# Last turn of two MLPs written out, and the norms behind them done inside the MLP stage

## The chip, the core and the metric

The kernel runs on one core of a Trainium2 chip. The metric is device time in microseconds (us), the median of several executions. Engines are named as in the profile: PE is TensorE's matrix multiplications, PEld its weight loads, DVE is VectorE, ACT is ScalarE, POOL is GpSimd, SP is the engine that issues most loads. Work on one engine runs in the order in which it is written; engines wait for each other only through semaphores.

## What is computed

A residual stream `x` of 256 rows by 1024 columns passes through a first network of two layers (attention, then a gated linear attention that is called gla below, each followed by a squared-ReLU MLP of width 4096) and a second network of two layers (a mix of attention and convolution, then a product-key mixture of experts). Of this, the change touches the end of each MLP and the norm behind it:

```python
def rmsnorm(x, g):
    y = x32 * lax.rsqrt(jnp.mean(x32 * x32, axis=-1, keepdims=True) + EPS)
    return (y * g.astype(jnp.float32)).astype(x.dtype)
...
        h = h + sq_relu_mlp(rmsnorm(h, norm_mlp[i]), mlp_w_in[i], mlp_w_out[i])
    return rmsnorm(h, final_norm)
...
        h = rmsnorm_2(x, norm1_g[l]) * (1.0 + sc1) + sh1
        proj = h @ w_in[l]
```

Behind the first MLP comes one norm (`norm_mix[1]`). Behind the second come two in a row: `final_norm`, whose result is the new `x`, and on it the first norm of the second network with its scale and shift.

## The kernel before

The kernel is a row of stages. Each has its own tiles and semaphores, and between two stages all engines meet in a barrier (L136). The 256 rows of `x` are two tiles (`t` = 0, 1) of 128 partitions. Weights come by SP in panels of 2 MB into a ring of four slots. A product of float32 accuracy is made of three passes (`three_passes`, L190 to L194): each operand is split into `hi`, a rounded copy by ACT, and `lo`, the rest, by DVE (`rest_of`, L187).

`mlp` (L414) handles the 32 chunks of 128 hidden columns in TURNS = 4 turns of CH = 8 chunks, in a hardware loop `Fori` on each engine. For a chunk `c`, `first(c)` multiplies the input weights with the turned input `hT` into the PSUM bank `hid[c % 2]` (24 matmuls of 256 columns). ACT takes the ReLU, DVE squares it to `act2`, ACT and DVE split that to `hidden`. `second(c)` multiplies `hidden` with the output weights into `acc`, four banks for tile and column half `(t, b)`, in 12 matmuls of 512 columns: three passes for each of the four `(t, b)`. PE's order is `first(c)`, `second(c - 2)`. The output weights of a chunk are split into buffer `c % 2` of `second_w`, so ACT waits until `second(c - 2)` has used it (the wait on `act_used` ahead of L566). `acc` starts with `x` itself (L509), so that it ends as the new residual stream.

Beside that, DVE sums rows for the conditioning of the second network (`condition`, L611), with rows that POOL loads, three in two chunks. After the last turn it stores them (`K.ada`, L628, L630), SP writes them out (L486), and in the second MLP DVE prepares the modulation row `K.mod[:, 0]` (L633). SP loads the next stage's four panels (`following`) as the slots fall free.

When the last `second` is done, ACT copies tile 1 of `acc` to `K.x` (L579) and DVE tile 0 (L636), and the stage ends. After the first MLP a stage `norm` (L235) follows: sum of squares of tile 1 on ACT and of tile 0 on DVE, mean, root, inverse, scaling by the gain row (L290), then for each of four halves (tile and column half) four PE transposes through PSUM (L309), ACT's `hi` (L273) and DVE's `lo` (L187) into `hT`. The next stage is `gla`. After the second MLP the stage `between_blocks` (L313, "bridge" in the trace) does two norms in a row: the same as `norm` up to the inverse, then `K.x` scaled (L357), the squares again (L339), mean, root, inverse again, the scaling by `K.mod[:, 0]` (L366), the shift by `K.mod[:, 1]` (L371), transposes (L384), `hi` (L345) and `lo`. The next stage is `mix`.

`Tail` (L642) is a norm done inside a stage: attention and gla end with it. There tile 0's norm is done while PE still sums tile 1, and tile 0's transposes are issued between the last matmuls of tile 1.

## Time and profile before

| | us |
|---|---|
| median of 3 runs | 2418.85 (2417.86 to 2419.85) |
| the profiled execution, device time | 2418.26 |
| its span, first to last instruction | 2416.6 |
| PE busy | 2112.2 (87%) |
| DVE busy | 1600.4 (66%) |
| ACT busy | 807.5 (33%) |
| mean granted clock of PE | 0.95 |
| the first MLP in the trace, with the norm behind it | 141.7 to 347.1 |
| the second MLP, with the two norms behind it | 504.7 to 712.3 |

All times in the rows are in microseconds from the start of the span. PE's granted clock is given as a share of full speed: 1.00 is the level of 2.4 GHz, 0.50 that of 1.2 GHz, a value between them a stretch that has both. The ends of matmuls are modelled, so distances between starts are safer than durations.

### The profile page before, as it was taken

Reading aid. Unit: us, or ns where it says so; the run is one execution under the profiler, and the core shown is the slowest. Engines: PE = TensorE matmul, PEld = TensorE weight load, DVE = VectorE, ACT = ScalarE, POOL = GpSimd, SP = SyncE. Lnnn points to the kernel's source line nnn. Section 1 sums busy time; section 2 is a strip of 40 time slices with the busy share of each in tenths; the row PEclk is TensorE's granted clock in tenths of the full one; section 3 lists DMA queues with packets and bytes.
Section 4 is the critical chain, followed back from the end, with each engine's and each line's share of the span. In section 5 each row is a group of like instructions: output and inputs, shape, how many; then the busy total and the mean of one; then the engine's idle time right before and its main releaser. Section 6 shows DMA issues by size and latency. Waiting matters only on the chain. (4 is left out here: it accounts for less than half of the span.)

```text
span 2416.6 us, 24918 instructions
## 1 busy us (share of the span) xinstructions
PE 2112.2 (87%) x8768; PEld 1363.8 (56%) x8768; DVE 1600.4 (66%) x3308; ACT 807.5 (33%) x1740; POOL 563.4 (23%) x604
## 2 busy tenths in 40 slices
PE   6689989989979999998788777899998988788777
PEld 5478877778969766554233333497664543333333
DVE  6567864577875658667766775656486676667655
ACT  4544435444445523221122112346232212121222
POOL 0000010000000203333333333102033333343332
PEclk9889989999989999999999989899999998898999
DMA  7068863178864449999999999864399999999997
GB/s 277 5 255 318 297 231 114 70 292 322 299 238 168 152 145 417 422 423 421 422 422 422 422 421 423 343 251 153 136 403 422 422 422 423 422 422 422 422 422 307
DMA packets 161333, 772.71 MB, mean 320 GB/s; under 512 B 12967, under 2 KB 13351, under 8 KB 89550
## 3 DMA queue, kind: packets, MB, share of 16 engines
q0 software_dynamic: 80640, 587.24, 59.1%
q1 hardware_dynamic: 80590, 184.17, 21.1%
q8 instruction: 56, 0.92, 0.2%
q14 instruction: 47, 0.39, 0.0%
HBM read 770.27 MB, written 1.10 MB: 319 GB/s over the span
## 5 line engine op out<-in xcount | busy, mean ns | idle before, releaser
L2667 ACT ACTIVATE experts_diagonal<-ident,experts_weight 128x128 f32<-128x128 f32 x488 | 155.9, 390 | 639.2 <-DVE experts_weight L2544 629.1
L2810 PE MATMUL experts_fourth<-ring,experts_diagonal 128*128 128x512 f32 x464 | 226.5, 638 | 45.0 <-ACT experts_diagonal L2667 41.7
L2288 POOL DMA_INDIRECT ring<-in_experts_uv_dram,experts_at x196 | 186.7, 953 | 305.3 <-PE experts_fourth L2810 142.1
L187 DVE TENSOR_TENSOR mix_lo<-ring,mix_hi 128x1024 fp32r<-128x1024 f32 (+1 forms) x98 | 132.5, 1358 | 118.2 <-ACT mix_hi L1962 115.1
L2489 DVE CUSTOM_DVE_ANT_0 ring<-ring,experts_second 128x1024 f32<-128x1024 f32 x116 | 141.6, 1220 | 96.5 <-DMA ring<-in_experts_uv_dram,experts_at 95.8
L2288 POOL DMA_INDIRECT experts_v_slot<-in_experts_uv_dram,experts_at x160 | 154.2, 964 | 204.5 <-PE experts_fourth L2810 108.1
L2810 PEld LDWEIGHTS experts_fourth<-ring,experts_diagonal 128*128 128x128 f32 x464 | 91.6, 203 | 176.4 <-issue 106.0
L2810 PE MATMUL experts_fourth<-experts_v_slot,experts_diagonal 128*128 128x512 f32 x320 | 156.2, 629 | 34.0 <-ACT experts_diagonal L2667 33.9
L2810 PE MATMUL experts_first<-ring,experts_diagonal 128*128 128x512 f32 x320 | 155.7, 636 | 33.5 <-ACT experts_diagonal L2667 33.5
L2810 PE MATMUL experts_first<-experts_v_slot,experts_diagonal 128*128 128x512 f32 x320 | 150.7, 611 | 13.5 <-ACT experts_diagonal L2667 13.4
L192 PE MATMUL mlp_hid<-mix_hT_hi,mlp_in_hi 128*128 128x256 f32 x512 | 147.2, 288 | 5.9 <-DVE mlp_in_lo L187 5.9
L494 POOL DMA_DIRECT2D mlp_ada_rows<-in_ada_turned_dram x48 | 25.6, 533 | 536.2 <-DVE mlp_turn_sums L611 315.7
L193 PE MATMUL mlp_hid<-mix_hT_lo,mlp_in_hi 128*128 128x256 f32 x512 | 146.0, 285 | 0.0
L194 PE MATMUL mlp_hid<-mix_hT_hi,mlp_in_lo 128*128 128x256 f32 x512 | 145.9, 285 | 0.0
L2489 DVE CUSTOM_DVE_ANT_0 experts_v_slot<-experts_v_slot,experts_second 128x1024 f32<-128x1024 f32 x80 | 97.6, 1221 | 69.2 <-DMA experts_v_slot<-in_experts_uv_dram,experts_at 68.7
L1962 ACT ACTIVATE mix_hi<-ring 128x1024 fp32r<-128x1024 f32 (+1 forms) x96 | 99.7, 1049 | 116.4 <-PE mix_sums L194 106.0
L2489 DVE CUSTOM_DVE_ANT_0 ring<-ring,experts_third 128x1024 f32<-128x1024 f32 x80 | 97.6, 1220 | 60.9 <-DMA ring<-in_experts_uv_dram,experts_at 60.2
L2489 DVE CUSTOM_DVE_ANT_0 experts_v_slot<-experts_v_slot,experts_third 128x1024 f32<-128x1024 f32 x80 | 97.5, 1219 | 57.3 <-DMA experts_v_slot<-in_experts_uv_dram,experts_at 56.4
L2810 PEld LDWEIGHTS experts_fourth<-experts_v_slot,experts_diagonal 128*128 128x128 f32 x320 | 63.5, 203 | 122.9 <-issue 74.9
L2810 PEld LDWEIGHTS experts_first<-ring,experts_diagonal 128*128 128x128 f32 x320 | 63.3, 202 | 115.8 <-issue 74.7
L611 DVE CUSTOM_DVE_ANT_0 mlp_ada_rows<-mlp_ada_rows,mlp_c_row 128x1024 f32<-128x1024 f32 x96 | 117.2, 1221 | 6.3 <-DMA mlp_ada_rows<-in_ada_turned_dram 6.3
L2662 ACT ACTIVATE experts_dots<-experts_dots 128x4 f32<-128x4 f32 x122 | 25.1, 205 | 278.5 <-DVE experts_dots L2489 278.4
(487 smaller groups left out, 4982.9 us busy)
## 6 DMA issues: line engine op xcount, KB each, us to landing
mlp_ada_rows<-in_ada_turned_dram POOLq DMA_DIRECT2D x48, 1024.0 KB, 5.4
ring<-in_w_in_dram SPq DMA_DIRECT2D x20, 2048.0 KB, 8.8
ring<-in_mlp_w_in_dram SPq DMA_DIRECT2D x16, 2048.0 KB, 9.8
ring<-in_mlp_w_out_dram SPq DMA_DIRECT2D x16, 2048.0 KB, 9.7
ring<-in_gla_w_in_dram SPq DMA_DIRECT2D x6, 2048.0 KB, 8.0
ring<-in_w_query_dram SPq DMA_DIRECT2D x6, 2048.0 KB, 8.0
ring<-in_w_out_dram SPq DMA_DIRECT2D x4, 2048.0 KB, 8.2
ring<-in_attn_w_qkv_dram SPq DMA_DIRECT2D x3, 2048.0 KB, 11.9
```

The costliest lines, as they stand in the source:

```text
L187: return dve.tensor_tensor(out_lo, a, hi.bitcast(F32), ALU.subtract)
L192: pe.matmul(out, at(lhs.hi), to(rhs.hi), start=start, stop=False, **more)
L193: pe.matmul(out, at(lhs.hi), to(rhs.lo), start=False, stop=False, **more)
L194: return pe.matmul(out, at(lhs.lo), to(rhs.hi), start=False, stop=stop, **more)
L494: pool.dma_start(ada_rows[:, slot, :, :], src).then_inc(ada_in[slot], 16)
L611: dve.tensor_tensor_reduce(a, a, c_row[:], 1.0, 0.0, ALU.mult, ALU.add, turn_sums[:, step:step + 1]).then_inc(summed, 1)
L1962: act.activation(w.hi[:, p % BUFFERS, begin:PIECE], K.ring[:, i % SLOTS, c * PIECE + begin:(c + 1) * PIECE], ACT.Copy).then_inc(hi_done, 1)
L2288: pool.indirect_dma_start(pair(i), None, rows, bass.IndirectOffsetOnAxis(ap=at[:, n, j:j + 1], axis=0)).then_inc(pair_in[slot_of(i)], 16)
L2489: dve.tensor_tensor_reduce(u_row(i), u_row(i), h2_ps[n // PH], 1.0, 0.0, ALU.mult, ALU.add, dots[:, n, j:j + 1]).then_inc(dots_done, 1)
L2662: act.activation(some, some, ACT.Gelu_apprx_tanh).then_inc(gelu_done, 1)
L2667: act.activation(diagonal[:, i % TOPK, :], K.ident[:], ACT.Copy, scale=weight[:, n, i % TOPK:i % TOPK + 1]).then_inc(diagonal_ready, 1)
L2810: mm = pe.matmul(y[n // PH][:, b, :], diagonal[:, j, :], v_row(i)[:, b * HALF:(b + 1) * HALF], start=n % PH == 0 and j == 0, stop=False, s ...
```

## The change

In both MLPs the loops run over three turns, and the fourth is written out. `second_w` has four buffers in place of two, in all turns. In the fourth turn PE does `second` for chunks 0 to 3 as before, but keeps chunks 4 to 7 until all of `first` is done. Then it goes through these four chunks for tile 0 (both column halves), again for tile 1's left half, and again for its right half.

A new class `Ending` does the norm or the norms in the MLP stage. It reads `acc` in PSUM where the stages before read `K.x`. With one norm (`again` false) the transposes of tile 0 are issued ahead of the last chunk's matmuls of tile 1; with two (`again` true) they follow all matmuls. With two norms, `K.x` first becomes `acc` times the gain row of the first norm ("weighed"), the second sum of squares is taken of that, and the first inverse is multiplied in later: into the second inverse for `hT` (`both`), and on ACT into `K.x` (`normalise`). The stages `norm` behind the first MLP and `between_blocks` go, with their barriers. DVE's preparation of `K.mod[:, 0]` stands ahead of the last turn, and so does its wait for the gain rows.

```diff
+class Ending:
...
+    def __init__(self, st, K, acc, hid, dead, hT, row, again):
+        self.K, self.acc, self.hid, self.hT, self.row, self.again = K, acc, hid, hT, row, again
+        self.more = st.ps("more", [P, 2, HALF])
+        self.xn = st.sb("xn", [P, T, D])
+        if again:
+            spare = st.sb("spare", [P, 2, HALF])
+            self.spare = [[a.rearrange("p a n -> p (a n)") for a in dead], [spare[:, h, :] for h in range(2)]]
...
+    def sums(self, t, f=0, n=D):
+        return self.acc[:, t, :, :].rearrange("p b n -> p (b n)")[:, f:f + n]
+
+    def bank(self, n):
+        return (self.hid, self.more)[n // 2][:, n % 2, :]
+
+    def transposes(self, pe, t):
+        for h in range(2):
+            pe.wait_ge(self.xn_done, 2 * t + h + 1)
+            for k in range(4):
+                f = (4 * h + k) * P
+                mm = pe.transpose(self.bank(2 * t + h)[:, k * P:(k + 1) * P], self.xn[:, t, f:f + P], self.K.ident[:])
+            mm.then_inc(self.turned, 1)
...
+    def scalar(self, act):
+        def square(t, part, n=HALF):
+            f = part * HALF
+            act.wait_ge(self.summed, 1 if t == 0 else 2 + part)
+            if self.again and (t, part) != (0, 1):
+                act.wait_ge(self.weighed, 1 if t == 0 else 3 + part)
+            to = self.spare[t][part] if self.again else self.xn[:, t, f:f + n]
+            act.activation(to, self.sums(t, f, n), ACT.Square,
+                           accum_out=self.ssq[:, 0, t, part:part + 1]).then_inc(self.squared, 1)
+
...
+        def normalise(t):
+            act.wait_ge(self.rstd_done, t + 1)
+            act.wait_ge(self.scaled, 2 * t + 2)
+            act.activation(self.K.x[:, t, :], self.K.x[:, t, :], ACT.Copy, scale=self.rstd[:, 0, t:t + 1])
+
+        if self.again:
+            square(0, 1)
+            square(0, 0)
+            square_weighed(0, 0, D, 0, 2)
+            root(0, 0, 1)
+            root(0, 1, 2)
+            square(1, 0)
+            square_weighed(1, 0, HALF, 0, 3)
+            normalise(0)
+            square(1, 1)
+            root(1, 0, 3)
+            high(0)
+            root(1, 1, 4)
+            high(1)
+            normalise(1)
+        else:
+            square(0, 0, D)
+            root(0, 0, 1)
+            square(1, 0)
+            act.wait_ge(self.xn_done, 2)
+            act.activation(self.K.x[:, 0, :], self.sums(0), ACT.Copy)
+            high(0)
+            high(1)
+            square(1, 1)
+            root(1, 0, 2)
+        high(2)
+        high(3)
+        if not self.again:
+            act.wait_ge(self.xn_done, 4)
+            act.activation(self.K.x[:, 1, HALF:D], self.sums(1, HALF, HALF), ACT.Copy)
...
+    def vector(self, dve, own):
+        def weigh(t, f, part):
+            dve.wait_ge(self.summed, 1 if t == 0 else 2 + part)
+            if (t, part) == (0, 1):
+                dve.wait_ge(self.squared, 1)
+            dve.tensor_tensor(self.K.x[:, t, f:f + HALF], self.sums(t, f, HALF), self.row[:, f:f + HALF],
+                              ALU.mult).then_inc(self.weighed, 1)
+
...
+        def mean_again(t, parts, squares):
+            dve.wait_ge(self.squared2, squares)
+            r = self.rstd[:, 0, t:t + 1]
+            own(dve.tensor_scalar(self.whole[:, 1, t:t + 1], total(1, t, parts), r, r, ALU.mult, ALU.mult))
+            dve.tensor_scalar(self.ms[:, 1, t:t + 1], self.whole[:, 1, t:t + 1], 1.0 / D, EPS, ALU.mult,
+                              ALU.add).then_inc(self.ms_done, 1)
...
+        if self.again:
+            weigh(0, 0, 0)
+            weigh(0, HALF, 1)
+            mean(0, 2, 2)
+            inverse(0, 0, 1)
+            mean_again(0, 1, 1)
+            inverse(0, 1, 2)
+            both(0)
+            scaled_again(0, 0)
+            weigh(1, 0, 0)
+            scaled_again(0, HALF)
+            weigh(1, HALF, 1)
+            square_weighed(1, HALF, 1)
+            mean(1, 2, 4)
+            shifted(0, 0)
+            inverse(1, 0, 3)
+            mean_again(1, 2, 2)
+            shifted(0, HALF)
+            inverse(1, 1, 4)
+            both(1)
+            scaled_again(1, 0)
+            scaled_again(1, HALF)
+            shifted(1, 0)
+            shifted(1, HALF)
+            low(0)
+            low(1)
+        else:
+            mean(0, 1, 1)
+            inverse(0, 0, 1)
+            scaled(0, 0)
+            scaled(0, HALF)
+            dve.wait_ge(self.squared, 2)
+            dve.tensor_copy(self.K.x[:, 1, 0:HALF], self.sums(1, 0, HALF))
+            low(0)
+            low(1)
+            mean(1, 2, 3)
+            inverse(1, 0, 2)
+            scaled(1, 0)
+            scaled(1, HALF)
+        low(2)
+        low(3)
...
+    BUFFERS = 4
+    HELD = CH - BUFFERS
...
-        first_w, second_w = (Parts(st.mem, nc, f"{st.name}_{n}", [P, 2, PIECE]) for n in ("in", "out"))
+        first_w, second_w = (Parts(st.mem, nc, f"{st.name}_{n}", [P, buffers, PIECE])
+                             for n, buffers in (("in", 2), ("out", BUFFERS)))
...
+        ending = Ending(st, K, acc, hid, (relu[:], act2[:]), hT, rows[0][0], scale is not None)
...
-                pe.sem_inc(act_used, LAG)
...
+                pe.sem_inc(act_used, BUFFERS)
...
+                def second(i, c, parts):
+                    pe.wait_ge(hidden_split, i * CH + c + 1)
+                    pe.wait_ge(out_split, i * CH + c + 1)
+                    for t, b in parts:
+                        mm = three_passes(pe, acc[:, t, b, :], hidden, second_w,
+                                          lambda x: x[:, c % 4, t * P:(t + 1) * P],
+                                          lambda x: x[:, c % BUFFERS, b * HALF:(b + 1) * HALF],
+                                          start=False, stop=False, skip_group_check=True)
+                    return mm
+
+                every = [(t, b) for t in range(T) for b in range(2)]
+                with pe.Fori(0, TURNS - 1) as i:
                     for c in range(CH + LAG):
                         if c < CH:
-                            first(c)
+                            first(i, c)
                         if c >= LAG:
-                            second(c - LAG)
+                            second(i, c - LAG, every).then_inc(act_used, 1)
+
+                last = TURNS - 1
+                for c in range(CH):
+                    first(last, c)
+                    if LAG <= c < HELD + LAG:
+                        second(last, c - LAG, every).then_inc(act_used, 1)
+                for c in range(HELD, CH):
+                    mm = second(last, c, every[0:2])
+                mm.then_inc(ending.summed, 1)
+                for c in range(HELD, CH):
+                    mm = second(last, c, every[2:3])
+                mm.then_inc(ending.summed, 1)
+                pe.wait_ge(relu_done, CH * TURNS)
+                for c in range(HELD, CH):
+                    mm = second(last, c, every[3:4])
+                    if c == CH - 2 and scale is None:
+                        ending.transposes(pe, 0)
+                mm.then_inc(ending.summed, 1)
+                if scale is not None:
+                    ending.transposes(pe, 0)
+                ending.transposes(pe, 1)
...
-                        act.wait_ge(act_used, i * CH + (c + 1 - 2 + LAG))
-                        act.activation(second_w.hi[:, c % 2, :], raw_out(g, m), ACT.Copy).then_inc(out_hi, 1)
...
+                    act.wait_ge(act_used, i * CH + c + 1)
+                    act.activation(second_w.hi[:, c % BUFFERS, :], raw_out(g, m), ACT.Copy).then_inc(out_hi, 1)
...
-                act.wait_ge(act_used, CH * TURNS + LAG)
-                act.activation(K.x[:, 1, :], acc[:, 1, :, :].rearrange("p b n -> p (b n)"), ACT.Copy)
...
+                with act.Fori(0, TURNS - 1) as i:
+                    turn(i)
+                turn(TURNS - 1)
+                ending.scalar(act)
...
+                with dve.Fori(0, TURNS - 1) as i:
+                    turn(i)
+                    keep(i)
+                dve.wait_ge(K.rows_in, 16 * len(rows))
                 if scale is not None:
                     dve.wait_ge(K.rows_in, 16 * (1 + len(rows)))
                     own(dve.scalar_tensor_tensor(out=K.mod[:, 0, :], in0=scale, scalar=1.0, in1=K.mod[:, 0, :],
                                                  op0=ALU.add, op1=ALU.mult))
-                dve.wait_ge(act_used, CH * TURNS + LAG)
-                own(dve.tensor_copy(K.x[:, 0, :], acc[:, 0, :, :].rearrange("p b n -> p (b n)")))
+                turn(TURNS - 1)
+                keep(TURNS - 1)
+                dve.tensor_tensor(K.ada[:, layer, :], K.ada[:, layer, :], ada_bias[:], ALU.add).then_inc(added, 1)
+                ending.vector(dve, own)
...
-    norm(nc, K, hT=hT, there=memory.shared[:, 0, :])
...
-    between_blocks(nc, K, A, memory)
```

Not shown: `first`, `rectify`, `square`, `condition` and the turns of ACT and DVE keep their content and take the turn as an argument.

## Rows read from the trace of the kernel before

**Rows 1.** Waits of PE, first MLP (engine, line waited for: us, times, longest).
```profile
PE mlp_hid L192 <- DVE mlp_in_lo L187: 4.2, 4, 3.2
PE mlp_acc L509 <- PEq L136: 2.3, 1, 2.3
```

**Rows 2.** Who waited for the tile `mlp_hidden_lo` in both MLPs (us in total, times).
```profile
PEld mlp_acc L192: 3.6, 8
```

**Rows 3.** Timeline of the first MLP's last turn: start, duration, engine, line, [idle before].
```profile
327.19 0.40 PE L192 MATMUL mlp_acc<-mlp_out_hi,mlp_hidden_hi 128*128 128x512 f32 x1
327.39 0.38 ACT L558 ACTIVATE mlp_relu<-mlp_hid 128x256 f32<-128x256 f32 x1 [1.50 <-PE mlp_hid L194]
...
329.94 0.39 PE L192 MATMUL mlp_acc<-mlp_out_hi,mlp_hidden_hi 128*128 128x512 f32 x1
330.14 1.06 ACT L566 ACTIVATE mlp_out_hi<-ring 128x1024 fp32r<-128x1024 f32 x1 [2.36 <-PE mlp_acc L194]
...
332.38 0.42 DVE L187 TENSOR_TENSOR mlp_hidden_lo<-mlp_act,mlp_hidden_hi 128x256 fp32r<-128x256 f32 x1
332.44 0.39 PE L194 MATMUL mlp_acc<-mlp_out_hi,mlp_hidden_lo 128*128 128x512 f32 x1
...
332.85 0.50 PE L192 MATMUL mlp_acc<-mlp_out_hi,mlp_hidden_hi 128*128 128x512 f32 x1
...
333.18 0.39 PE L193 MATMUL mlp_acc<-mlp_out_lo,mlp_hidden_hi 128*128 128x512 f32 x1
```

**Rows 4.** Timeline from the first MLP's last matmul to gla's first.
```profile
335.48 0.39 PE L194 MATMUL mlp_acc<-mlp_out_hi,mlp_hidden_lo 128*128 128x512 f32 x1
...
347.14 0.37 SPq L850 DMA_DIRECT2D gla_wz<-in_gla_w_in_dram  x1
...
350.05 0.80 PE L192 MATMUL gla_sums<-gla_hi,mix_hT_hi 128*128 128x512 f32 x1 [5.04 <-DVE gla_lo L187]
```

**Rows 5.** Timeline from the second MLP's last matmul to mix's first.
```profile
694.57 0.39 PE L194 MATMUL mlp_acc<-mlp_out_hi,mlp_hidden_lo 128*128 128x512 f32 x1
...
695.07 1.23 DVE L636 COPY x<-mlp_acc 128x1024 f32<-128x1024 f32 x1 [1.55 <-PE mlp_acc L194]
697.27 1.03 ACT L333 ACTIVATE bridge_tp<-x 128x1024 f32<-128x1024 f32 x1 [1.26 <-PEq L136]
...
701.82 1.03 ACT L339 ACTIVATE bridge_tp<-x 128x1024 f32<-128x1024 f32 x1
...
703.00 0.17 DVE L360 TENSOR_SCALAR bridge_ms<-bridge_ssq 128x2 f32<-128x2 f32 x1 [1.21 <-ACT bridge_tp L339]
703.20 0.20 ACT L342 ACTIVATE bridge_std<-bridge_ms 128x2 f32<-128x2 f32 x1 [0.23 <-DVE bridge_ms L360]
703.43 0.17 DVE L362 RECIPROCAL bridge_rstd<-bridge_std 128x2 f32<-128x2 f32 x1 [0.27 <-ACT bridge_std L342]
703.63 1.42 DVE L366 SCALAR_TENSOR_TENSOR bridge_xn<-x,bridge_rstd,mod 128x512 f32<-128x512 f32 x2
...
707.49 1.29 DVE L371 TENSOR_TENSOR bridge_xn<-bridge_xn,mod 128x512 f32<-128x512 f32 x2
...
712.34 0.34 SPq L1816 DMA_DIRECT2D mix_conv_cols<-in_conv_turned_dram  x1
```

**Rows 6.** Timeline of attention's tail, which norms tile 1 inside its stage.
```profile
131.55 1.03 PE L682 MATMUL attn_more<-ident,mod 128*128 128x128 f32 x8
...
135.22 0.63 ACT L689 ACTIVATE shared<-x 128x512 f32<-128x512 f32 x1 [1.46 <-DVE x L717]
...
135.98 0.21 DVE L721 TENSOR_SCALAR attn_tail_ms<-attn_tail_ssq 128x1 f32<-128x1 f32 x1 [0.79 <-ACT shared L689]
136.23 0.15 DVE L723 TENSOR_SCALAR attn_tail_ms<-attn_tail_ms 128x1 f32<-128x1 f32 x1
...
140.03 0.69 DVE L187 TENSOR_TENSOR mix_hT_lo<-attn_more,mix_hT_hi 128x512 fp32r<-128x512 f32 x1 [0.35 <-ACT mix_hT_hi L698]
```

**Rows 7.** Stretches: us, busy us of PE, PEld, DVE, ACT, POOL, granted clock, DMA share, GB/s.
```profile
350.00:353.50 3.50, 3.46 (x8) 2.81 (x9) 2.98 (x4) 2.80 (x3) 3.14 (x6) 0.50 0.14 44
```

275 lines of the change are left out of this document (126 added, 149 removed).

## The prediction

> **What bounds the kernel now.** I read the views in this order: the busy shares, the waits of PE inside an MLP, the timeline of an MLP's last turn, and then the timeline from its last matmul to the first matmul of the next stage. The shares say that PE is busy 87% of the span, but that is an average, and the change touches two places only.
>
> Inside the MLPs PE is the bound. From the start of the first MLP to its end PE's matmuls wait 4.2 us for split input weights, 3.2 of it once at the start, and 2.3 us at the entry barrier, and for nothing else [rows 1]. A further, small wait is booked to the weight loads: eight times, once in each turn of both MLPs, 3.6 us in total, for the `lo` part of the hidden chunk [rows 2]. What it costs is read from the distances between matmul starts. Ahead of the last `second`, the distance from L194 to L192 is 332.85 - 332.44 = 0.41 us and the next one 333.18 - 332.85 = 0.33, where the pitch is (329.94 - 327.19) / 12 = 0.229 [rows 3]. So one such wait costs 0.41 + 0.33 - 0.46 = 0.28 us. Its cause stands in the same rows: the split of the last output chunk (L566) starts at 330.14, after ACT had waited 2.36 us for PE to free one of two buffers, though the ReLU of that chunk had begun at 327.39.
>
> Behind the MLPs the norms are the bound, and PE stands still. From the last matmul's end (335.48 + 0.39 = 335.87) to the first instruction of gla (347.14) it is 11.27 us [rows 4]. From the second MLP's last matmul's end (694.96) to the first instruction of mix (712.34) it is 17.38 us [rows 5]. Both stretches lie whole on the path, as no engine has work of another stage in them. So the gain to be had is what of these 28.65 us can be done beside PE's own last matmuls, plus two of the barriers, plus the eight small waits.
>
> **The small waits.** With four buffers the split of output chunk 7 needs no release by PE. It can start when ACT is through with its ReLU, at about 327.39 + 0.3 instead of 330.14. `hidden_lo`, which ended near 332.8, then ends 2 us earlier or more and before PE comes to it at 332.67. All eight waits go: 8 x 0.28 = 2.2 us, 1.1 for each MLP. What is late next is PE itself, whose chunk pair takes 24 + 12 matmuls whatever the buffers do. In the written-out turn the order is different, so I check it apart. Let F be the end of the last `first`. PE goes straight on with chunks 4, 5 and 6 for tile 0, three times 6 x 0.229 = 1.37 us, and comes to chunk 7 at F + 4.1. DVE must by then have done, from the ReLU of chunk 6 on (F - 2.7, because the last two `first` now run back to back): a square, two condition sums, two output splits, a second square and two hidden splits. With the waits for ACT in between I come to F + 3.8. That is 0.3 us of slack: I cost this at nothing, and if the slack is gone it costs the difference, at most the 0.28 of before.
>
> **The end of the first MLP.** Let Z be the time when tile 0 is complete, after 4 x 6 x 0.229 = 5.5 us of held chunks. The remaining matmuls of tile 1 take another 5.5 us, so PE's sums without any insertion would end at Z + 5.5, which is the point that answers to 335.87. Tile 0: square of 1024 columns, mean, root, inverse, and two scalings take 1.2 + 0.63 + 2 x 0.71 = 3.3 us (lengths as in [rows 5]: 701.82 to 703.00, 703.00 to 703.63, and the halves of 1.42). PE comes to tile 0's transposes at Z + 4.8, so they wait for nothing. The eight transposes cost PE 1.03 us, read from attention's tail, which issues eight in the same place [rows 6]. The last sum is thus ready at Z + 6.55. From here on tile 1 is alone, and attention's tail shows this very chain: from the square of the last half (135.22) to the end of the last `lo` (140.03 + 0.69) it takes 5.50 us [rows 6]. The stage ends near Z + 12.1. The barrier I take as the one between the second MLP and the bridge, 696.30 to 697.27, 0.97 us [rows 5]. gla starts at Z + 13.1, that is 7.6 us after the point that answers to 335.87, against 11.27 before. Gain 3.65 us.
>
> **The end of the second MLP.** Here tile 0's chain is longer. Up to the first scaling by the product of both inverses: a weighing of 0.7, the second one with its square behind the first (to Z + 1.5), the square of the weighed tile (1.2), root, inverse, two small operations, root, inverse, the product (0.2 to 0.25 each by [rows 5, 6]): Z + 4.3. Then DVE's list goes: scale, weigh, scale, weigh (2 x 0.71 + 2 x 0.69) and a sum of squares of half a tile (0.75): Z + 7.9. ACT needs until Z + 8.95 for its two squares, `normalise` of tile 0 (1.0) and the last square (0.76), so DVE waits 1.1 us here. The second mean takes 0.4, shift 0.65, five small operations 0.9, shift 0.65, two more 0.5, giving Z + 12.1; scale twice (1.4), shift twice (1.3) and four `lo` (4 x 0.68 = 2.7) bring Z + 17.5. Transposes and `hi` run beside these. With 0.97 for the barrier mix starts at Z + 18.5, which is 13.0 us after PE's sums, against 17.38. Gain 4.4 us. Of that, what the trace of before does not show is how often DVE and ACT wait for each other in this new order. The bound from below is DVE without any wait: 1.1 us here and about 2 us ahead of Z + 4.3 fall away, 3 us better. The bound from above is another 0.27 us (the hand-over from ACT to DVE in [rows 5]) at each of some nine crossings, 2.5 us worse. I take the middle, as the list itself is fixed and its lengths are measured.
>
> **What is moved.** The preparation of `K.mod[:, 0]`, 1.2 us of DVE, now stands between turns three and four. DVE has just gained 2 us there, as its last `lo` of the turn no longer waits, so PE does not see it. Without that cover it would cost up to 1.2 us once. Its wait for the rows has nothing queued that matters: they were loaded at the start of the stage. SP's four panel loads and the store of `K.ada` hang on the splits, which come 2 us earlier. The last store is issued with nothing behind it. POOL's loads wait for the condition sums, which are not held up. The copies of `acc` to `K.x` (about 1 us each, ACT and DVE) leave the path; ACT's last one runs beside the last `lo`.
>
> **The barrier** after an MLP with nothing shorter ahead of it may be 0.8 to 1.4 us instead of 0.97. That is -0.2 to +0.4 for each.
>
> **The sum.** 2 x 1.1 + 3.65 + 4.4 = 10.3 us. The profiled execution took 2418.26, so 2408.0. It lies 0.59 us under the median of the runs shown, so the median should be 2408.6.
>
> **The code itself.** Each turn back in the loop is a jump. The starts of PE's matmuls show no idle time at any of them: the only waits of PE between the second turn and the end are for data [rows 1, 2]. By the Trainium skill (Runtime: NRT & Kernel Launch, Instruction fetch mechanics) fetching is sequential, and a taken jump to a page outside the window stalls. By it the change would save one such stall for each MLP and engine, and written-out code would cost nothing; the row has zero for the stall, so the sum stays as it is either way.
>
> **Rivals.**
> (a) *The second ending is bound by its order.* DVE and ACT hold each other up at each step of the interleaved list, for instance a root that sits on ACT behind a `hi` that waits for transposes. At most its whole gain of 4.4 us is given back: 2413.0. For it speaks that DVE's list has no free work to fill a wait with; against it that every piece is shorter than the one it replaces.
> (b) *The four buffers don't do what they say.* The eight waits stay, since the split of the hidden chunk hangs on ReLU and square and not on the buffer: 2408.6 + 2.2 = 2410.8. Against it: the 2.36 us wait in [rows 3].
> (c) *The clock stays up.* gla's first 3.5 us run at a granted clock of 0.50 [rows 7], from its first matmul at 350.05 on, after PE had been nearly idle since 335.87. If the shorter pause keeps the clock at 1.00, half of that is saved, 1.75 us, and about as much at mix: 2405. Against it: PE still pauses for more than 5 us ahead of gla's first matmul (2.9 us of it inside gla, 347.14 to 350.05).
> (d) *Slower: the written-out turn starves for instructions.* Behind the loop each engine runs into code that it has not run before, while DMA is loaded with panels. The nearest row for a sequencer that is not ready is 2.3 us at the stage's entry [rows 1]. The gain is used up when such a stall hits PE more than four times in total (10.3 / 2.3); with four in each MLP, one for each two `first`, it is 8 x 2.3 - 10.3 = 8.1 us slower: 2427. Against it: the rest of the kernel is straight code of the same kind, and PE's matmuls in it wait for data.
>
> **How the numbers follow.** Forecast 0.67, (a) 0.13, (b) 0.10, (c) 0.06, (d) 0.04. Around 2408.6 the bounds are: second ending -3 and +2.5, barriers -0.4 and +0.8, the product-key stages' own variation about 1 us as in the three runs. They do not all fall on one side, so 2404 to 2411.5 for the forecast alone; (a) and (b) are taken in up to 2413. Range 2404 to 2413. The limit of what can be told from no change is 0.2%, 4.8 us, so faster means under 2414.0. That holds for the forecast, (b), (c) and nearly all of (a): 0.92. Same 0.04, slower 0.04.
>
> **What would show it.** In the profile after: no wait of PE's weight loads for `mlp_hidden_lo` but perhaps in the last turn; the stretch from PE's last sum of the first MLP to gla's first instruction near 6.5 us (7.6 less the inserted transposes), and from that of the second MLP to mix's first near 13; the time from mix's start to the end of the span unchanged within 1 us. Wrong would be: an idle PE between the last `first` and the held chunks, a wait of DVE of more than 1.5 us in the second ending, or a stage behind that grows by what was gained.

## The result, and the profile after

The changed kernel takes 2406.49 us (2405.42 to 2408.01) against 2418.85 of the kernel before in the same runs: a ratio of 0.995, 95% interval 0.9939 to 0.996. That is 12.4 us less; the interval of the ratio stands for 9.7 to 14.8. The profiled execution took 2405.89, 12.37 less than that of before. The forecast was 10.3 less, 2408.6. The time lies inside the range, and the sign was right.

The page of the kernel after begins so (span; then busy time of an engine, its share and its instructions):

```profile
span 2404.1 us, 24851 instructions
...
PE 2102.4 (87%) x8768; PEld 1358.2 (56%) x8768; DVE 1597.4 (66%) x3321; ACT 807.4 (34%) x1755; POOL 564.8 (23%) x604
```

To see where the time went, I cut both profiled executions at the first instruction of each stage. All numbers are us; "before" and "after" are the two profiles.

| stretch | before | after | difference |
|---|---|---|---|
| first MLP's first matmul to gla's first instruction | 205.44 | 198.28 | -7.16 |
| gla | 157.56 | 157.58 | +0.02 |
| second MLP to mix's first instruction | 207.64 | 201.54 | -6.10 |
| mix to the end of the span | 1704.26 | 1705.00 | +0.74 |

The gain sits in the two MLPs and is not given back behind them. Inside an MLP the starts of the ReLUs cut it finer, since there is one for each output chunk. "Turn 1, chunk 1 to turn 3, chunk 6" holds two of the three turn ends, the row ahead of it the other one. The last column but one is the whole ending, up to the next stage's first instruction, with the last turn's own small wait in it.

| MLP | stage start to the third ReLU | third ReLU to turn 1, chunk 1 | to turn 3, chunk 6 | to the next stage | sum |
|---|---|---|---|---|---|
| first, before | 20.09 | 42.36 | 117.62 | 25.37 | 205.44 |
| first, after | 17.89 | 42.03 | 117.03 | 21.33 | 198.28 |
| second, before | 16.14 | 42.40 | 117.62 | 31.48 | 207.64 |
| second, after | 16.29 | 42.04 | 117.03 | 26.18 | 201.54 |

**The turns.** These are the two ReLUs around the end of turn 0 in the first MLP (start, duration, line, operation; in brackets the idle time ahead of it), first of before, then of after:

```profile
189.90 0.38 ACT L558 ACTIVATE mlp_relu<-mlp_hid 128x256 f32<-128x256 f32 x1 [1.50 <-PE mlp_hid L194]
201.28 0.38 ACT L558 ACTIVATE mlp_relu<-mlp_hid 128x256 f32<-128x256 f32 x1 [5.37 <-PE mlp_hid L194]
```
```profile
187.69 0.38 ACT L699 ACTIVATE mlp_relu<-mlp_hid 128x256 f32<-128x256 f32 x1 [3.98 <-PE mlp_hid L194]
198.75 0.38 ACT L699 ACTIVATE mlp_relu<-mlp_hid 128x256 f32<-128x256 f32 x1 [7.53 <-PE mlp_hid L194]
```

The distance falls from 11.38 to 11.06, 0.32 us a turn end. The waits of PE's matmuls and weight loads in the first MLP of after answer to [rows 1] and [rows 2] (time in total, times, longest):

```profile
PE mlp_hid L192 <- DVE mlp_in_lo L187: 4.0, 4, 3.2
...
PE mlp_more L363 <- DVE mlp_xn L457: 2.4, 1, 2.4
...
PE mlp_hid L192 <- ACT mlp_relu L699: 0.4, 1, 0.4
```
```profile
PEld mlp_hid L192 <- DVE mlp_in_lo L187: 5.5, 4, 3.4
...
PEld mlp_more L363 <- DVE mlp_xn L457: 3.1, 2, 2.8
```

No wait for `mlp_hidden_lo` is left in either list.

**The first ending.** The timeline of after, from the last `first` on. It answers to [rows 3] and [rows 4]:

```profile
321.33 0.40 PE L192 MATMUL mlp_acc<-mlp_out_hi,mlp_hidden_hi 128*128 128x512 f32 x1
...
326.80 0.39 PE L192 MATMUL mlp_acc<-mlp_out_hi,mlp_hidden_hi 128*128 128x512 f32 x1
327.00 1.03 ACT L373 ACTIVATE mlp_xn<-mlp_acc 128x1024 f32<-128x1024 f32 x1 [2.95 <-PE mlp_acc L194]
...
331.56 1.03 PE L363 MATMUL mlp_hid<-ident,mlp_xn 128*128 128x128 f32 x8
...
332.89 0.40 PE L194 MATMUL mlp_acc<-mlp_out_hi,mlp_hidden_lo 128*128 128x512 f32 x1
333.33 0.60 ACT L373 ACTIVATE mlp_xn<-mlp_acc 128x512 f32<-128x512 f32 x1
...
338.11 0.69 DVE L187 TENSOR_TENSOR mix_hT_lo<-mlp_more,mix_hT_hi 128x512 fp32r<-128x512 f32 x1 [0.42 <-ACT mix_hT_hi L387]
339.98 0.37 SPq L1004 DMA_DIRECT2D gla_wz<-in_gla_w_in_dram  x1
```

From 321.33 to 326.80 PE starts 24 held matmuls in 5.47 us, 0.228 each, so it does not starve in the written-out part. Z is again the time when tile 0 is complete, the end of the last of these 24. It is 326.97, and the tile is squared at once, while PE still has 5.5 us of tile 1 ahead. The transposes of tile 0 wait for nothing. The last `lo` ends at 338.80 = Z + 11.8, and gla starts at Z + 13.0.

**The second ending.** Its timeline, which answers to [rows 5], and two of the waits of DVE from Z = 681.26 on:

```profile
681.30 1.49 DVE L431 TENSOR_TENSOR x<-mlp_acc,shared 128x512 f32<-128x512 f32 x2 [1.49 <-PE mlp_acc L194]
...
685.42 0.75 DVE L467 SCALAR_TENSOR_TENSOR mlp_xn<-x,mlp_whole,mod 128x512 f32<-128x512 f32 x1
...
688.07 1.14 ACT L393 ACTIVATE x<-x,mlp_rstd 128x1024 f32<-128x1024 f32 x1
...
689.11 0.58 ACT L373 ACTIVATE mlp_spare<-mlp_acc 128x512 f32<-128x512 f32 x1
...
689.88 0.16 DVE L437 TENSOR_TENSOR mlp_whole<-mlp_ssq 128x1 f32<-128x1 f32 x1 [1.11 <-ACT mlp_spare L373]
...
691.79 0.60 ACT L387 ACTIVATE mix_hT_hi<-mlp_hid 128x512 fp32r<-128x512 f32 x1 [1.32 <-PE mlp_hid L363]
692.28 0.19 ACT L383 ACTIVATE mlp_std<-mlp_ms 128x1 f32<-128x1 f32 x1
692.51 0.16 DVE L447 RECIPROCAL mlp_rstd<-mlp_std 128x1 f32<-128x1 f32 x1 [0.32 <-ACT mlp_std L383]
...
697.61 0.69 DVE L187 TENSOR_TENSOR mix_hT_lo<-mlp_more,mix_hT_hi 128x512 fp32r<-128x512 f32 x1 [0.16 <-ACT mix_hT_hi L387]
699.10 0.34 SPq L1968 DMA_DIRECT2D mix_conv_cols<-in_conv_turned_dram  x1
```
```profile
DVE mlp_rstd L447 <- ACT mlp_std L383: 1.5, 3, 0.9
...
DVE mlp_whole L437 <- ACT mlp_spare L373: 1.1, 1, 1.1
```

The last `lo` ends at 698.30 = Z + 17.0, and mix starts at Z + 17.8. The written order costs in two places. DVE stands 1.1 us because ACT's `normalise` of tile 0 (688.07) is queued ahead of the last square (689.11). Then it stands 0.32 us for tile 1's second root (692.28): its mean was ready at 691.59, but on ACT the root is queued behind the first `hi` of tile 0 (691.79), and that waits for PE's transposes. How long they take hangs on the clock. These are the four transposes of after, then of the kernel with the later `normalise`, which is among the experiments:

```profile
690.88 0.87 PE L363 MATMUL mlp_hid<-ident,mlp_xn 128*128 128x128 f32 x4 [4.18 <-DVE mlp_xn L473]
```
```profile
691.14 0.66 PE L363 MATMUL mlp_hid<-ident,mlp_xn 128*128 128x128 f32 x4 [3.21 <-DVE mlp_xn L473]
```

In after the granted clock falls from 1.00 to 0.50 while they run, and they take 0.87 us; in the other profile it falls later, they take 0.66, and DVE does not wait for that root.

**What is left over.** Turn ends and endings give 1.87 + 4.04 + 5.30 = 11.2 us. The last piece is the first turn of the first MLP, 20.09 against 17.89, and this piece the change does not explain. In these two profiles PE idles there once for 3.2 us, for a split input weight. In both kernels the reason is the same: DVE's first condition sum stands in front of that split and waits for its rows. The timeline of after, then three stretches of before and two of after (us, busy time and instructions of PE, PEld, DVE, ACT, POOL, then the granted clock, DMA share, GB/s):

```profile
151.11 1.23 DVE L756 CUSTOM_DVE_ANT_0 mlp_ada_rows<-mlp_ada_rows,mlp_c_row 128x1024 f32<-128x1024 f32 x1 [3.91 <-DMA mlp_ada_rows<-in_ada_turned_dram]
...
152.26 1.22 DVE L187 TENSOR_TENSOR mlp_in_lo<-ring,mlp_in_hi 128x1024 fp32r<-128x1024 f32 x1
```
```profile
152.00:153.30 1.30, 0.03 (x1) 0.03 (x1) 1.30 (x4) 0.35 (x1) 0.00 (x0) 0.54 0.05 19
153.30:155.00 1.70, 1.70 (x8) 1.70 (x9) 1.70 (x4) 0.42 (x1) 0.00 (x0) 0.50 0.02 5
155.00:157.00 2.00, 2.00 (x11) 2.00 (x11) 2.00 (x3) 0.00 (x0) 0.53 (x1) 0.50 0.47 66
```
```profile
153.30:155.00 1.70, 1.47 (x12) 1.47 (x13) 1.70 (x5) 0.42 (x1) 0.00 (x0) 1.00 0.02 5
155.00:157.00 2.00, 2.00 (x19) 2.00 (x19) 2.00 (x2) 0.29 (x2) 0.53 (x1) 1.00 0.14 25
```

In before TensorE comes back from the pause at a granted clock of 0.50, its lower level of 1.2 GHz, and starts 11 matmuls in 2 us; in after it stays at 1.00, 2.4 GHz, and starts 19. Whether that belongs to the change is a question for the experiments.

### The profile page after: what moved, and what is told of

Its sections match the earlier page's. It is cut to its first block and busy times, and to the rows that moved or that the text cites. A ratio compares the mean times of both kernels' runs of the same rounds, so it can differ in the third digit from the quotient of the medians.

```text
span 2404.1 us, 24851 instructions
## 1 busy us (share of the span) xinstructions
PE 2102.4 (87%) x8768; PEld 1358.2 (56%) x8768; DVE 1597.4 (66%) x3321; ACT 807.4 (34%) x1755; POOL 564.8 (23%) x604
## 5 line engine op out<-in xcount | busy, mean ns | idle before, releaser
L2962 PE MATMUL experts_fourth<-ring,experts_diagonal 128*128 128x512 f32 x464 | 220.9, 625 | 47.5 <-ACT experts_diagonal L2819 44.1
```

Of the source, the lines that this page charges most:

```text
L2962: mm = pe.matmul(y[n // PH][:, b, :], diagonal[:, j, :], v_row(i)[:, b * HALF:(b + 1) * HALF], start=n % PH == 0 and j == 0, stop=False, s ...
```

## The experiments

My theory: the gain has three independent parts (four buffers, tile 0's norm under tile 1's matmuls, stages dropped), and the clock in the first turn is chance. Rivals: the recorded (a), (b) and (d); that dropping the stages is the gain and the held chunks are not; and that the first turn's clock belongs to the change. Eleven runs follow: nine new kernels, and each of the two once more. Each has the kernel before beside it on the same chip, and every ratio is taken to that one and not to the 2418.85 of the result. Its medians there were 2421.77 us for the first four runs, 2419.35 for the next four and 2418.91 for the last three. The ratio is an estimate from all executions, so it can differ a little from the quotient of the medians.

### Four buffers alone

```diff
-    first_w, second_w = (Parts(st.mem, nc, f"{st.name}_{n}", [P, 2, PIECE]) for n in ("in", "out"))
+    first_w, second_w = (Parts(st.mem, nc, f"{st.name}_{n}", [P, buffers, PIECE])
+                         for n, buffers in (("in", 2), ("out", 4)))
...
-    act.wait_ge(act_used, i * CH + (c + 1 - 2 + LAG))
+    act.wait_ge(act_used, i * CH + c + 1)
```

> The kernel before with four buffers for the split output weights in place of two, and nothing else of the change. Theory (the small wait in each turn is ACT waiting for a buffer): the eight waits go, each 0.3 us, so 2.4 us faster than before, a median near 2416.4. The distance between the ReLU of chunk 7 and that of the next turn's chunk 0 falls from 11.38 to 11.06 us. Rival (the hidden chunk's split hangs on ReLU and square, not on the buffer): no change, within 0.5 us of before, and 11.38 stays. Also open: whether PE's clock falls in the first turn of the first MLP, as it did in the profile before (8.72 us from the ReLU of chunk 0 to that of chunk 1) and did not in the profile after (6.29); if the drop hangs on chance, it may be there or not in each run, worth 2.4 us.

Measured: 2417.57 us, ratio 0.9985 (0.9977 to 0.9994), that is 1.5 to 5.6 us less than before. The turns do what they do in after: chunk 7 to the next chunk 0 takes 11.06, and the long stretch falls from 117.62 to 116.97 and 116.98. The endings fall by 0.31 and 0.32 (to 25.06 and 31.16), which is the last turn's own wait. That is 2.6 us in all by these stretches. The first turn is left out of that sum: in the second MLP of this profile PE has a pause of 2.8 us there, and the third ReLU comes at 19.34 us where before has 16.14. So rival (b) falls: the waits hung on the buffer.

### The last turn written out, nothing else new

```diff
+    for c in range(CH + LAG):
+        if c < CH:
+            first(TURNS - 1, c)
+        if c >= LAG:
+            second(TURNS - 1, c - LAG, every).then_inc(act_used, 1)
```

> Four buffers and the fourth turn written out on PE, ACT and DVE in the same order as in the loop; the copies to x, the norm stage and the bridge as before. Theory (straight code costs what looped code costs): the same as with four buffers alone, 2.4 us faster than before, within 1 us of that run. Rival (the written-out turn starves for instructions): slower than that run by at least 2.3 us for each stall, with PE idle in the last turn without a wait for data.

Measured: 2417.52 us, ratio 0.9984 (0.9975 to 0.9992), the same as with the four buffers alone. The stretch with the border between loop and written-out code is 117.04 in both MLPs, against 116.97: at most 0.07 us for the border. In the list of PE's waits in the first MLP one thing is new, 0.4 us at chunk 2 of the last turn for a ReLU (`mlp_hid` from `mlp_relu`); it stands where the four-buffer kernel has its fourth small wait for an input split, so it replaces that one, and the 0.07 us is what is left of it. Rival (d) falls.

### One MLP at a time

The other MLP keeps its old code and the norm stage behind it. The edit of the first of the two kernels:

```diff
-    mlp(nc, K, hT, A.mlp_w_in[1], A.mlp_w_out[1], conditions(1), following=wide(A.w_in_2[0], range(SLOTS)),
+    mlp_plain(nc, K, hT, A.mlp_w_in[1], A.mlp_w_out[1], conditions(1), following=wide(A.w_in_2[0], range(SLOTS)),
...
+    between_blocks(nc, K, A, memory)
```

> The whole change in the first MLP, the second MLP and the bridge as before. Theory: 1.0 us for the turns' ends and 4.0 for the ending, so 5.0 us faster, a median near 2413.9 (2411.5 if the clock drop of the first turn goes with the change and does not hang on chance). Rival (the second ending carries the gain, the first only moves it): under 2 us faster.

> The whole change in the second MLP, the first MLP and the norm stage as before. Theory: 1.0 us for the turns' ends and 5.2 for the ending, so 6.2 us faster, a median near 2412.7; with the run for the first MLP the two gains add up to 11.2, and the rest of the measured 12.4 is chance of the clock. Rival (something in the later stages takes part of it): the stretch from the start of mix to the end of the span grows by over 1 us against before.

Measured: the first MLP alone 2413.41 us, 0.9969 (0.9957 to 0.9981); the second alone 2418.16 us, 0.9986 (0.9977 to 0.9994). The first is 4.6 to 10.4 us less than before, where 5.0 was expected. The second is 1.5 to 5.6 less, where 6.2 was expected, and that is a miss. By its profile the second MLP gains in full (207.64 to 201.65), the first one ends as in before (25.37), and mix to the end takes 1704.37 us as against 1704.26, so the recorded rival is not it. gla, which neither version touches, took 159.87 instead of 157.56, 2.3 us more; that is taken up in the last section. But the profiled execution took 2413.22 us and was the fastest of eleven, so it can't say why their median is 5 us higher. Some 0.5 us lies outside the span: device time less span is 2.1 us in both of these kernels, 1.6 in before and 1.8 in after. The rest of the miss stays open. What the profiles do show is that each MLP's gain is its own and that they add: turn ends and ending give 4.9 us in the first kernel and 6.1 in the second, against 11.2 in after.

### Tile 0 not held back

All four quarters of a chunk together, as in the loop, with the new endings:

```diff
-    for c in range(HELD, CH):
-        mm = second(last, c, every[0:2])
-    mm.then_inc(ending.summed, 1)
...
+    for c in range(CH + LAG):
+        if c < CH:
+            first(last, c)
+        if c >= LAG:
+            mm = second(last, c - LAG, every)
+            mm.then_inc(act_used, 1) if c - LAG < CH - 1 else mm.then_inc(ending.summed, 3)
```

> The kernel after, but in the last turn each chunk's second product is done for all four parts at once in the loop's order, so that both tiles are complete at the same time; the norms stay in the MLP stage and read PSUM. Theory (most of the gain is the overlap of tile 0's norm with PE's sums of tile 1): the first ending loses 4.8 us and the second 5.5, together 10.3 slower than after, a median near 2416.8. Rival (most of the gain is the two stages, barriers and copies that go): it keeps more than half of the gain, a median under 2411.

Measured: 2417.83 us, ratio 0.9997 (0.9988 to 1.0006). Nearly the whole gain is gone. Its first ending shows why:

```profile
332.79 1.02 ACT L373 ACTIVATE mlp_xn<-mlp_acc 128x1024 f32<-128x1024 f32 x1 [6.55 <-PE mlp_acc L194]
...
343.00 0.69 DVE L187 TENSOR_TENSOR mix_hT_lo<-mlp_more,mix_hT_hi 128x512 fp32r<-128x512 f32 x1 [0.16 <-ACT mix_hT_hi L387]
344.87 0.37 SPq L994 DMA_DIRECT2D gla_wz<-in_gla_w_in_dram  x1
```

The same chain of steps now begins with the square of tile 0 only when all sums are there, and takes 12.1 us from 332.79 to gla. The two endings take 25.88 and 31.89 us, where the old norm stages with four buffers took 25.06 and 31.16. So doing the norms in the MLP stage without an overlap is 0.7 to 0.8 us worse for each MLP than two stages with a barrier between them. Of the 0.8 us in the first ending, 0.4 is the longer barrier there (1.18 us against 0.79). The rival that the dropped stages are the gain falls: holding tile 1 back is the gain, 4.55 and 5.71 us. The three parts of my theory are not independent, though. The held chunks need the four buffers, and they pay only because the norm stands in the same stage; held chunks with the norm stages kept were not run.

### The condition sums behind the first chunks

The theory of the first turn says that the 3.2 us pause comes from DVE's queue. So the condition sum is moved behind the split that PE waits for, in chunks 1 and 2 of each turn:

```diff
-    if 0 < c <= CH:
+    if 2 < c <= CH:
         condition(i, step)
     if c < CH:
         first(i, c)
+    if 0 < c <= 2:
+        condition(i, step)
```

> The kernel after, with DVE's condition sum of the positions c = 1 and c = 2 of each turn put behind the split of the input weights. Theory (PE's wait of 3.2 us in the first turn and of 0.4 us at the start of each later turn is DVE busy with, or waiting for the rows of, a condition sum): the 3.2 us wait shrinks to under 1, the later ones vanish, the clock can't fall there any more; 4 to 5 us faster than after, near 2402. Rival (the sum that is put off comes back later as a wait for the hidden chunk, since DVE has 5.2 us of work in each 5.6): within 1 us of after.

Measured: 2408.55 us, ratio 0.9952 (0.9938 to 0.9965), no better than after. The theory is missed, and the recorded rival is what came. The first pause is gone: the first two ReLUs are 2.87 us apart. The price is in every turn. These are the ReLUs of chunks 0 to 3 of turn 1:

```profile
196.80 0.38 ACT L699 ACTIVATE mlp_relu<-mlp_hid 128x256 f32<-128x256 f32 x1 [7.53 <-PE mlp_hid L194]
199.67 0.39 ACT L699 ACTIVATE mlp_relu<-mlp_hid 128x256 f32<-128x256 f32 x1 [0.29 <-PE mlp_hid L194]
203.84 0.37 ACT L699 ACTIVATE mlp_relu<-mlp_hid 128x256 f32<-128x256 f32 x1
209.00 0.39 ACT L699 ACTIVATE mlp_relu<-mlp_hid 128x256 f32<-128x256 f32 x1 [0.98 <-PE mlp_hid L194]
```

In after chunk 1 to 2 takes 3.56 (201.62 to 205.18) and chunk 2 to 3 5.54. Here they take 4.17 and 5.16, together 0.23 more, and three turns make the 117.72 of this kernel out of 117.03. One step later DVE is late again, for chunk 2.

### The normalise two places later

```diff
-            normalise(0)
             square(1, 1)
             root(1, 0, 3)
+            normalise(0)
             high(0)
```

> The kernel after, with ACT's last square of the second ending ahead of its scaling of tile 0 of x. Theory (DVE waits 1.1 us for that square, and behind it the second ending is DVE's list alone): 1.0 us faster than after, the last lo of that ending at 16.0 us behind the start of its first square in place of 17.0. Rival (the scaling then holds up the hi of tile 0 or the second root, and DVE waits there): within 0.3 us of after.

> The kernel after with both of these edits. Theory: the gains add, 5 to 6 us faster than after, near 2401, and faster than before by about 18. Rival (one of the two is no gain, as told with them): the time of the better of the two alone.

Measured with this one edit: 2406.02 us, 0.9946 (0.9932 to 0.9959). The median can't tell this from after; the profile can. From turn 3, chunk 6 to the last `lo` of the second MLP it is 24.26 instead of 25.38, and the 1.1 us wait is gone from DVE's list:

```profile
DVE x L431 <- PE mlp_acc L194: 1.4, 1, 1.4
DVE mlp_rstd L447 <- ACT mlp_std L383: 1.2, 2, 0.9
DVE mix_hT_lo L187 <- ACT mix_hT_hi L387: 0.2, 1, 0.2
```

Of these 1.1 us the edit itself gives 0.9. The other 0.2 is the wait for tile 1's second root, which a clock that falls later shortens: the second profile of after, with the old order, has 25.15.

Both edits together: 2407.88 us, 0.9951 (0.9938 to 0.9965). That is a miss, since 5 to 6 us less than after were expected. The later sums take back 0.68 us in each MLP's long stretch. The second ending has 24.94, which is 0.7 more than with the later `normalise` alone, but only 0.2 of that comes with the sums, as a later start of the ending. For the rest the clock is at 0.50 for all of the first four transposes (1.11 us instead of 0.66), and DVE waits behind them:

```profile
693.44 0.17 DVE L447 RECIPROCAL mlp_rstd<-mlp_std 128x1 f32<-128x1 f32 x1 [0.56 <-ACT mlp_std L383]
```

A kernel with that root ahead of the `hi` was not run.

### Both kernels again, and the best version

> The kernel before once more, for a second profile of it. Theory (PE's clock in the first turn of the first MLP hangs on chance and not on the change): the distance between the first two ReLUs lies somewhere between 5.7 and 8.8 us, as in the eight runs so far whose first turn differs in nothing that bears on it; all stretches that have no clock change in them are the same as in the first profile within 0.1 us (42.4 us from the ReLU of chunk 2 in turn 0 to that of chunk 1 in turn 1, 117.6 from there to chunk 6 of turn 3, 24.6 and 30.7 from there to the end of the norms). Rival (the drop belongs to the kernel before): 8.7 again.

> The kernel after once more, on the same chip as the two others of this call. Theory: 11 to 12.5 us faster than before; in the profile the same stretches as in the first one (20.2 and 25.4 us from the ReLU of chunk 6 in turn 3 to the end of the norms), and a distance between the first two ReLUs anywhere from 5.7 to 8.8. Rival: 6.3 again, and before 8.7 again, so that the change owns the difference.

> The kernel after with ACT's last square of the second ending ahead of its scaling of x, and DVE's condition sum behind the split of the input weights at position c = 1 of each turn only, not at c = 2. Theory (at c = 1 DVE has slack in every turn but the first, where the sum waits for its rows; at c = 2 it has none): turns 1 to 3 keep 42.0 and 117.0 us, the first two ReLUs come 2.9 us apart, the next distance grows by about 2, together 1 us for each MLP's start besides the 1.1 of the square and what the clock gives; near 2404. Rival (the wait only moves one chunk on, as it did with both sums put off): the sum of the first two distances is not shorter than in a run of after without the clock drop, 5.7 + 2.9 = 8.6 us.

The kernel before, sent as its own rival: 2419.35 us, 1.0001 (0.9993 to 1.001). Its first two ReLUs are 4.86 us apart, where the other profile of the very same program has 8.72, and its granted clock stays at 1.00 in the stretch where that one had 0.50:

```profile
153.30:155.00 1.70, 1.70 (x17) 1.70 (x16) 1.70 (x3) 0.32 (x2) 0.15 (x1) 1.00 0.01 5
155.00:157.00 2.00, 2.00 (x19) 2.00 (x18) 2.00 (x4) 1.10 (x2) 0.38 (x1) 1.00 0.46 86
```

4.86 is below the 5.7 that I had set as the lower end, so the size was missed. One reason is that the pause itself was shorter: PE waited 1.7 us here and 3.2 in the first profile, because DVE waited 2.5 us for its rows and not 4.0. So this pair alone mixes two things, 1.5 us of pause and 2.4 us of clock. The stretches without a clock change came back as expected (42.37, 117.62, 24.59 and 30.73 us). The kernel after again: 2406.71 us, 0.9951 (0.9939 to 0.9963). Its first two ReLUs are 7.08 apart, against 6.29, though its pause is shorter, 2.5 us against 3.2, because now the clock falls in after too:

```profile
153.30:155.00 1.70, 1.70 (x10) 1.70 (x10) 1.70 (x3) 0.25 (x1) 0.06 (x1) 0.50 0.01 5
```

So the drop belongs to neither program. The two endings of after came back 0.2 us shorter than in the first profile (19.96 and 25.15 to the last `lo`), with fewer of the transposes at the lower clock.

The last version combines the later `normalise` with the one condition sum that causes the pause (chunk 1 only):

```diff
-    if 0 < c <= CH:
+    if 1 < c <= CH:
         condition(i, step)
     if c < CH:
         first(i, c)
+    if c == 1:
+        condition(i, step)
```

Measured: 2404.90 us (2401.76 to 2407.66), ratio 0.9938 (0.9926 to 0.995). This is the lowest median of all, 1.8 us under the changed kernel beside it, though the two intervals overlap. Its first three ReLUs in the first MLP:

```profile
151.00 0.38 ACT L699 ACTIVATE mlp_relu<-mlp_hid 128x256 f32<-128x256 f32 x1 [7.14 <-PE mlp_hid L194]
153.87 0.38 ACT L699 ACTIVATE mlp_relu<-mlp_hid 128x256 f32<-128x256 f32 x1 [0.30 <-PE mlp_hid L194]
158.58 0.37 ACT L699 ACTIVATE mlp_relu<-mlp_hid 128x256 f32<-128x256 f32 x1
```

From the first to the third it is 7.58 us. The second distance grew by 1.8 us, as the theory had it, and the rival, which wanted at least 8.6 us for the two, falls. In the three kernels with this sum moved it is 7.08 to 7.58, in the nine others that kept it in front 7.74 to 10.27, and 11.71 in the first profile of before. The later turns stay as in after (117.04), and the second ending has the 24.3 of the later `normalise`. So the placement of that one sum is worth 0.2 to 4 us in this stretch, depending on the clock and on the length of the pause. From the start of the stage to the third ReLU the second profile of before (16.75 us) is level with the three (16.64 to 16.88). In this profile gla gives 3 us of it back (160.63); see the last section. So the profile shows the gain in the second ending, but not that moving the sum lowered the median.

## Why the prediction was right

The forecast had the mechanism and the place of each part. The differences are sizes, and one small wait that its list of steps did not have.

- **The small waits.** Forecast 8 x 0.28 = 2.2 us. By the stretches it is 1.87 for the six turn ends inside (0.31 each) and 0.31 + 0.32 in the endings of the four-buffer kernel, 2.5 in all. The way of reading the cost, from distances between matmul starts, was right; it saw 0.28 of 0.31.
- **The written-out turn.** Costed at nothing, with a slack of 0.3 us for chunk 7. The four held chunks run at 0.228 us a matmul without a hole, and the kernel that only writes the turn out loses 0.07 us at most. This step holds.
- **The first ending.** Forecast 3.65 without the small wait. Between the four-buffer kernel and after it went from 25.06 to 21.33: 3.73. The inner points: last `lo` at Z + 11.8 (forecast 12.1), gla at Z + 13.0 (13.1). The last sum was ready 0.2 us earlier than forecast and the barrier took 1.18 us, not 0.97, so the two errors cancel; that the forecast met this term within 0.1 us is partly luck. The second profile of after has 21.14. From PE's last sum (333.29) to gla it is 6.7 us, where I said near 6.5.
- **The second ending.** Forecast 4.4, measured 31.16 - 26.18 = 4.98. This is the most mis-sized term of the sum. The first scaling came at Z + 4.15 (4.3), the last square's mean at Z + 8.6 (8.95), the list's end at Z + 17.0 (17.5), and the barrier took 0.80 (0.97); both barriers lie in the forecast's 0.8 to 1.4. ACT was through with its four pieces earlier than I had summed them. The 1.1 us wait of DVE was foretold and is there with 1.1; moving one call took it away. The 0.3 us wait behind the `hi` was not in the list of steps. From PE's last sum (686.70) to mix it is 12.4 us, where I said near 13.
- **What is moved.** The preparation of `K.mod[:, 0]` shows nowhere: the stretch that holds it is 117.03 in the second MLP of after, and 117.03 too in the first one, which has no such preparation. No wait for a DMA or for POOL's loads is new in the lists above.
- **The stages behind.** Forecast unchanged within 1 us, measured +0.02 and +0.74. Over all twelve other profiles, the stretch from mix to the end lies between 1703.7 and 1707.8, so +0.74 says nothing.
- **The sum.** 2.5 + 3.73 + 4.98 = 11.2 against 10.3. The profiled pair shows 12.4, of which about 2.2 is the first turn of the first MLP, less 0.9 in the other stretches. The medians' interval, 9.7 to 14.8 us, holds both 10.3 and 11.2 and can't decide between them. That the profiled pair and the medians both show 12.4 is no confirmation of either sum.

**The rivals.** (a), the second ending bound by its order: two such places exist, 1.1 and 0.3 us. The second is the very example that the rival gave, a root on ACT behind a `hi` that waits for transposes, and it takes 0 to 0.6 us as the clock has it. But the ending gained more than forecast in spite of both. (b), the buffers without effect: refuted by the four-buffer kernel. (c), the clock stays up behind a shorter pause: refuted. gla's first 3.5 us have the same clock as in [rows 7], by this row of after:

```profile
342.90:346.40 3.50, 3.50 (x8) 2.82 (x9) 1.61 (x2) 2.58 (x4) 2.95 (x9) 0.50 0.18 49
```

At mix it is the same: the first 3.5 us of its matmuls have a granted clock of 0.50 in before (713.8 to 717.3) and in after (700.6 to 704.1).

(d), starving for instructions: refuted by the written-out kernel, whose PE has no hole at the border. The rule of the Trainium skill that I had set beside it (Runtime: NRT & Kernel Launch, Instruction fetch mechanics: straight code is fetched ahead, a taken jump can stall) agrees for straight code, 0.07 us at most. A stall per turn back, which the change would have saved once an MLP, is not seen: writing the last turn out gained nothing over the loop.

## What to carry to other kernels

Where a reduction over everything follows a matmul-bound stage, reorder the last pieces so that one output tile is complete early, and put its whole chain under the matmuls of the other one; here the held tile was worth 10.3 us, and merging the stages without it cost 1.5. To price a wait that is booked at weight loads, measure the distance from start to start of the matmuls around it, and compare it to the pitch. On an in-order engine, look at what stands in front of the short instruction that another engine waits for: one call moved by two places was worth 0.9 us, a root behind a copy that waits for another engine cost up to 0.6, and a sum that waits for a DMA in front of a needed split cost up to 4, clock included.

## What the runs showed of the hardware

- **The clock after a short pause varies from one execution to the next.** In the ten profiles with the condition sum in front, PE pauses in the first turn at the same place, for 1.7 to 3.2 us, as the rows of that sum land earlier or later. Behind the pause the granted clock stays at 1.00 in six of them and falls to 0.50 in four. The length of the pause does not decide it: in after it stays behind 3.2 us and falls behind 2.5; over all ten it falls behind 2.4, 2.5, 2.8 and 3.2 us and stays behind 1.7, 2.5, 2.7, 2.7, 2.8 and 3.2. What decides it is not shown. A single profiled pair can show 4 us of difference in a stretch that nobody changed.
- **The clock falls inside the new endings.** PE has little to do there, and the last transposes run at 1.00, at 0.50 or across the change. In the first ending the eight of tile 1 take 1.32 us in the kernel with the later `normalise` and 1.77 in after, and the endings are 20.88 and 21.33 us long. So two endings that differ by less than 0.5 us may differ by the clock alone.
- **The clock comes back at different times.** In the profiles of before, of after and of the kernel with the later sums, gla begins at 0.50. In after the clock is back 3.5 us behind gla's first matmul (346.40). In the kernel with the later sums it is not, at the same distance:

```profile
345.40:346.90 1.50, 1.50 (x5) 1.16 (x4) 0.95 (x1) 0.00 (x0) 1.36 (x3) 0.50 0.00 0
346.90:348.40 1.50, 1.50 (x10) 1.11 (x9) 0.00 (x0) 0.00 (x0) 0.54 (x3) 0.71 0.54 70
```

  There gla took 160.09 us, and in four of the thirteen profiles it took 159.9 to 160.6, against 157.6 to 158.4 in the nine others. The long ones are those in which the clock comes back late: 8.1 to 8.8 us behind gla's first instruction, against 5.8 to 7.8 in the nine others. Three of the four are just the three kernels with a sum moved; the fourth is the one with only the second MLP changed, whose first MLP is that of before. So it happens without a moved sum, but that a moved sum makes it more likely is not excluded. This stays open; it would take more profiles of the same kernels.
- **The barrier between two stages had a price of its own at each place.** From the last `lo` to the next stage's first instruction it is 0.78 to 0.80 us behind the second MLP's norms in all kernels, 1.18 to 1.19 behind the first one's new ending and 0.78 to 0.79 behind its old one. What makes the 0.4 us was not tried. ACT's copy of `x` ends at 337.97 + 0.59 = 338.56, ahead of the last `lo`, so it is not the late one.
